# Two fillings of 96 and 32 bytes ahead of a transformer kernel's row buffers and second memory area

## The chip, the cores and the metric

The kernel runs on one core of a Trainium2 chip. The metric is the device time of one execution in microseconds. Before the change it is 1265.22 us, the median of three runs (1264.64 to 1267.24).

## What is computed

Two transformer blocks, one after the other, over 256 tokens of width 1024. The first has an mLSTM mixer and a layer of 16,384 experts (PEER); the second has a mixer of attention and a linear recurrence, and a plain MLP. The part that matters here is the expert layer. For each token and each of 8 heads, 16 experts are chosen, and each expert is one row of `u` and one of `v`:

```python
def block(args):
    hb, eb, gb = args
    ub = jnp.take(u, eb, axis=0)
    z = jnp.einsum('thkd,td->thk', ub, hb)
    a = (jax.nn.gelu(z.astype(jnp.float32)) * gb).astype(hb.dtype)
    return jnp.einsum('thk,thkd->td', a, jnp.take(v, eb, axis=0))
```

That is 256 x 128 rows of `u` and as many of `v`, all float32, 268 MB in all.

## The kernel before

It is written by hand with a program for each engine and semaphores between them. There are three stages that matter here.

**First block's mixer (to about 330 us).** SyncE streams the weights in loads of 1 MB (128 partitions x 8,192 bytes), most of them into five ring buffers `ring0` to `ring4`; three of the first loads go to `ya`, `qkT` and `pad`, which are not in use yet. ScalarE (L1073) and VectorE (L1550) split each chunk into a high and a low part, `halves`, and TensorE multiplies them with `hh` and `hl` (L496, L497, L500).

**Expert layer (about 320 to 965 us).** `peer_uv` holds for each expert its row of `u` and its row of `v` side by side, 8,192 bytes. GpSimd issues 256 gathers (L2398, the last three in two parts at L2407), each an indirect DMA of one expert for each of 128 tokens, so 1 MB into one row buffer. For each row buffer VectorE multiplies the `u` half with the token's `h2t` and sums (`dot`, L2042), ScalarE applies the gelu and writes a diagonal matrix `dg` (L1356), and TensorE adds the `v` half to the output in two products, which the trace has as two passes each (L858). There are 17 row buffers, in a list `row_places`:

```python
row_places = [gbuf[:, j, :] for j in range(4)] + [wq_places[j][:, :] for j in w_free[0:2]] + [ring[UV_SLOTS[2]][:, :]]
row_places += [gbuf[:, j, :] for j in range(4, 8)]
row_places += [row_place[:, :], ring[A0][:, :], ring[A1][:, :], wq_places[w_free[2]][:, :]]
row_places += [ring[j][:, :] for j in UV_SLOTS[0:2]]
```

So buffers 0 to 3 and 7 to 10 lie in `gbuf`, 4, 5 and 14 are the three `wq_place`, 11 is `row_place`, and 6, 12, 13, 15 and 16 are ring buffers. A table `ROW_SLOT` sets which gather goes where. From gather 94 to gather 157 its cycle has 16 gathers, in the order 4, 5, 8, 13, 14, 9, 0, 10, 15, 1, 2, 3, 6, 11, 7, 12; from gather 158 on buffer 16 stands behind 10 and the cycle has 17, to 216, where buffer 11 leaves. Three in each cycle go to a `wq_place`, one to `row_place`. A gather is issued as soon as TensorE is done with the row that the buffer held (semaphore `s_comb`). Of the 256 rows 50 go to the `wq_place` buffers, 15 to `row_place`, 126 to `gbuf` and 65 to the ring.

**Second block (965 us to the end).** Weights again through the ring, split into `half2_*`, and multiplied with `hf2`, `mxh`, `gh` and so on (L1017, L1020, L1047 to L1049).

SBUF tensors lie one behind the other in each partition, in the order in which the program names them, and each starts at a multiple of 32 bytes. Those named through `sb(...)` keep their place for the whole program. Behind them lies an area that is laid out anew for each stage (`st(...)`, given back by `stage.close()`): first the mixer's tiles, then the expert layer's, then the second block's.

Of the kernel before, what the change touches and what calls it, by code (L numbers as in the profile page):

```python
# [130 lines left out]
def build_program(nc, A, out):  # L131
# [6 lines left out]
    def sb(name, shape, dt=f32):  # L138
        return ctx.enter_context(nc.sbuf_tensor(name, shape, dt))
# [135 lines left out]
    iota16 = sb("iota16", [128, 16])  # L275
    mneg = sb("mneg", [128, 128], bf16)
    identb = sb("identb", [128, 128], bf16)
    banks = [ctx.enter_context(nc.psum_tensor(f"bank{i}", [128, 512], f32)) for i in range(8)]

    stage = ExitStack()  # L280

    def st(name, shape, dt=f32):
        return stage.enter_context(nc.sbuf_tensor(name, shape, dt))
# [38 lines left out]
    sct = st("sct", [128, 2, 4, 128])  # L322
    pk = st("pk", [128, 1088])
    rx = st("rx", [128, 3, 40])
    pku = st("pku", [128, 64], u32)
    ei = st("ei", [128, 2, 128], u32)
    za = st("za", [128, 2, 32])
# [2180 lines left out]
```

## Time and profile before

| | |
|---|---|
| median of three runs | 1265.22 us |
| the profiled execution: time | 1264.27 us |
| the profiled execution: span | 1262.5 us |
| TensorE matmul busy | 1142.1 us (90%) |
| VectorE busy | 919.4 us (73%) |
| ScalarE busy | 511.4 us (41%) |
| GpSimd busy | 328.7 us (26%) |
| moved by DMA | 406.70 MB, 322 GB/s over the span |

The span is the time from the first to the last instruction of the profiled execution. A share of 90% for TensorE is an average over stages: whether TensorE sets the time has to be read stage by stage, from the busy shares in slices or stretches of the span and from what the DMA engines do in the same stretch.

### The profile page before, as it was taken

What the parts mean: (1) busy time and instruction counts of PE and PEld (TensorE: products, weight loads), DVE (VectorE), ACT (ScalarE), POOL (GpSimd) and SP (SyncE); (2) the same over time, 40 slices, a digit from 0 to 9 for tenths busy, and PEclk for the clock granted to TensorE, in tenths of its full rate; (3) what the DMA queues carried; (4) which work ended last, traced back from release to release, by engine and by line L of the source; (5) the groups of instructions that cost most, each with busy time, mean ns of one, the idle gap of its engine ahead of it and who ended that gap; (6) DMA issues with size and microseconds to landing.
All of it is one profiled execution on the core that took longest, in us unless ns stands there. A gap on an engine that the chain in (4) does not pass through costs nothing.

```text
span 1262.5 us, 14930 instructions
## 1 busy us (share of the span) xinstructions
PE 1142.1 (90%) x5180; PEld 797.5 (63%) x5180; DVE 919.4 (73%) x1848; ACT 511.4 (41%) x992; POOL 328.7 (26%) x316
## 2 busy tenths in 40 slices
PE   5999999999899998988778878887789999999998
PEld 4989999998655454443333433332335897788887
DVE  5997987786869667777677766677756696888544
ACT  3657443554423222221222222221524477677442
POOL 4000000000446444544454454454433000000000
PEclk9999999999999999999998999899989999999999
DMA  8874577588999999999999999999997622555550
GB/s 352 335 283 185 179 293 279 208 318 325 363 424 393 426 424 426 426 426 425 426 426 426 425 426 426 426 426 425 427 423 309 232 101 73 195 195 176 197 200 34
DMA packets 58703, 406.70 MB, mean 322 GB/s; under 512 B 7012, under 2 KB 7220, under 8 KB 10500
## 3 DMA queue, kind: packets, MB, share of 16 engines
q0 software_dynamic: 39184, 273.55, 51.9%
q1 hardware_dynamic: 19444, 132.19, 28.3%
q8 instruction: 42, 0.69, 0.2%
q14 instruction: 33, 0.27, 0.1%
HBM read 404.66 MB, written 1.06 MB: 321 GB/s over the span
## 4 chain that ended last, share of the span: by engine, by line
PE 58%; DMA 25%; DVE 9%; issue 4%; ACT 3%; POOL 1%; SPq 0%; DVEq 0%; POOLq 0%; ACTq 0%
PE bank L858 15%; DMA row_place<-in_peer_uv,ei 8%; DMA ring<-in_peer_uv,ei 6%; PE bank L496 5%; PE bank L500 5%; PE bank L497 5%; DMA gbuf<-in_peer_uv,ei 5%; PE bank L1017 5%; DMA wq_place<-in_peer_uv,ei 4%; PE bank L781 3%; PE bank L1020 2%; PE bank L1047 2%; PE bank L1048 2%; PE bank L1049 2%; PE bank L521 2%
## 5 line engine op out<-in xcount | busy, mean ns | idle before, releaser
L858 PE MATMUL bank<-gbuf,dg 128*128 128x512 f32 x504 | 247.2, 632 | 60.2 <-ACT dg L1356 58.1
L1550 DVE TENSOR_TENSOR half<-ring,half 128x1024 fp32r<-128x1024 f32 x175 | 212.7, 1222 | 85.1 <-ACT half L1073 83.1
L1073 ACT ACTIVATE half<-ring 128x1024 fp32r<-128x1024 f32 x173 | 181.7, 1055 | 126.4 <-PE bank L1049 47.0
L858 PEld LDWEIGHTS bank<-gbuf,dg 128*128 128x128 f32 x504 | 98.1, 200 | 193.9 <-issue 112.6
L2042 DVE CUSTOM_DVE_ANT_0 gbuf<-gbuf,h2t 128x1024 f32<-128x1024 f32 x126 | 154.4, 1225 | 72.2 <-DMA gbuf<-in_peer_uv,ei 68.1
L2398 POOL DMA_INDIRECT gbuf<-in_peer_uv,ei x123 | 140.4, 1141 | 172.7 <-PE bank L858 107.7
L1348 ACT ACTIVATE za<-za 128x4 f32<-128x4 f32 x62 | 12.7, 205 | 401.9 <-DVE za L2042 401.9
L858 PE MATMUL bank<-ring,dg 128*128 128x512 f32 x260 | 131.1, 633 | 17.3 <-ACT dg L1356 13.0
L496 PE MATMUL bank<-hh,half 128*128 128x256 f32 x448 | 113.1, 290 | 0.6 <-DVE hl L1708 0.3
L2042 DVE CUSTOM_DVE_ANT_0 ring<-ring,h2t 128x1024 f32<-128x1024 f32 x65 | 79.7, 1225 | 46.5 <-DMA ring<-in_peer_uv,ei 43.9
L497 PE MATMUL bank<-hl,half 128*128 128x256 f32 x448 | 110.5, 284 | 0.0
L858 PEld LDWEIGHTS bank<-ring,dg 128*128 128x128 f32 x260 | 53.0, 207 | 88.1 <-issue 70.0
L2398 POOL DMA_INDIRECT ring<-in_peer_uv,ei x65 | 82.3, 1266 | 93.5 <-PE bank L858 44.0
L858 PE MATMUL bank<-wq_place,dg 128*128 128x512 f32 x200 | 96.5, 619 | 9.6 <-ACT dg L1356 6.8
L1356 ACT ACTIVATE dg<-ident,za 128x128 f32<-128x128 f32 x256 | 83.1, 391 | 40.4 <-DVE za L2053 29.9
L2398 POOL DMA_INDIRECT wq_place<-in_peer_uv,ei x50 | 59.1, 1181 | 111.3 <-DVE ei L1968 66.6
L496 PEld LDWEIGHTS bank<-hh,half 128*128 128x128 f32 x448 | 86.5, 193 | 1.5 <-issue 0.8
L497 PEld LDWEIGHTS bank<-hl,half 128*128 128x128 f32 x448 | 86.5, 193 | 0.5 <-issue 0.5
L2042 DVE CUSTOM_DVE_ANT_0 wq_place<-wq_place,h2t 128x1024 f32<-128x1024 f32 x50 | 60.9, 1224 | 22.0 <-DMA wq_place<-in_peer_uv,ei 20.1
L858 PEld LDWEIGHTS bank<-wq_place,dg 128*128 128x128 f32 x200 | 38.8, 197 | 59.0 <-issue 49.7
L1017 PE MATMUL bank<-hf,half 128*128 128x512 f32 x256 | 64.9, 394 | 0.1
L500 PE MATMUL bank<-hh,half 128*128 128x256 f32 x448 | 62.9, 283 | 0.0
(446 smaller groups left out, 1999.7 us busy)
## 6 DMA issues: line engine op xcount, KB each, us to landing
ring<-in_weights SPq DMA_DIRECT2D x116, 1024.0 KB, 5.3
gbuf<-in_weights SPq DMA_DIRECT2D x4, 1024.0 KB, 9.8
gbuf<-in_peer_uv,ei POOLq DMA_INDIRECT x129, 14.8
bcs<-in_b_ada POOLq DMA_DIRECT2D x3, 512.0 KB, 12.3
ring<-in_peer_uv,ei POOLq DMA_INDIRECT x65
xs<-in_x SPq DMA_DIRECT2D x2, 512.0 KB, 4.0
ya<-in_weights SPq DMA_DIRECT2D x1, 1024.0 KB, 18.0
qkT<-in_weights SPq DMA_DIRECT2D x1, 1024.0 KB, 20.0
```

The costliest lines, as they stand in the source:

```text
L496: e.matmul(pb[:, 0:256], hi[:, k, :], xh[:, k, :], start=k == 0, stop=False)
L497: e.matmul(pb[:, 0:256], hi[:, k, :], xl_[:, k, :], start=False, stop=False)
L500: r = e.matmul(pb[:, 0:256], lo[:, k, :], xh[:, k, :], start=False, stop=k == 7)
L521: r = e.matmul(two[a][:, :], xh[:, k, 128 * a:128 * a + 128], lo[:, k - k0, :], start=False, stop=stop and k > k0)
L781: r = e.matmul(pb[:, s_], v[:, k, :], hf[:, k, s_], start=k == 0, stop=k == 7)
L858: r = e.matmul(acc[a][j][:, :], dg[:, i % 4, :], expert_rows(i)[:, 1024 + 512 * j:1536 + 512 * j], start=h == 0 and k == 0, stop=h == 7 an ...
L1017: e.matmul(pb[:, :], hi[:, k, :], hf2[:, :, k, :], start=k == 0, stop=False)
L1073: e.activation(h, v, AF.Copy).then_inc(*o.inc(*highs_of(n)))
L1356: e.activation(dg[:, i % 4, :], ident[:, :], AF.Copy, scale=za[:, i // 16 % 2, 16 + i % 16:17 + i % 16]).then_inc(*o.inc(s_dg, i + 1))
L1550: e.tensor_tensor(l, v, h.bitcast(f32), ALU.subtract).then_inc(*o.inc(s_lov, split(n)))
L2042: e.tensor_tensor_reduce(row, row, h2t[:, ITS[n][0], :], 1.0, 0.0, ALU.mult, ALU.add, za[:, n % 2, i % 16:i % 16 + 1]).then_inc(*o.inc(s_d ...
L2398: e.indirect_dma_start(out=expert_rows(i), out_offset=None, in_=A["peer_uv"], in_offset=bass.IndirectOffsetOnAxis(ap=ei[:, a, at:at + 1], ...
```

## The change

Two tensors are added that no instruction reads or writes.

```diff
     identb = sb("identb", [128, 128], bf16)
+    sb("to_line0", [128, 24])
     banks = [ctx.enter_context(nc.psum_tensor(f"bank{i}", [128, 512], f32)) for i in range(8)]
...
     rx = st("rx", [128, 3, 40])
+    st("to_line1", [128, 8])
     pku = st("pku", [128, 64], u32)
```

The first takes 96 bytes of each partition, behind the lasting tensors; everything of the three stages' area moves up by 96 bytes. The second takes 32 bytes between `rx` and `pku` in the expert layer's area; what lies behind it there moves by 128 bytes in all. No instruction is added, removed or reordered on any engine or queue, and no size changes. What changes is where tensors start in a partition. The offset of the start from a multiple of 256 bytes, before and after:

| tensors | before | after |
|---|---|---|
| `ring0` to `ring4`, `xs`, `bc0`, `bcs`, `ident`, `masks` | 128 | 128 |
| `wq_place0` to `2` (row buffers 14, 4 and 5), `row_place` (buffer 11) | 32 | 128 |
| `gbuf` (row buffers 0 to 3 and 7 to 10), `dg`, `ei` | 0 | 128 |
| `hf`, `h2t`, `qT`, `skT`, `sct`, `pk` | 32 | 128 |
| first mixer: `halves`, `hh`, `hl`, `yh`, `yl`, `pad` | 32 | 128 |
| first mixer: `cg`, `qkT`, `vx`, `wo_half*` | 160 | 0 |
| first mixer: `ya`, `xn`, `scr`, `accd`, `nb` | 224 | 64 |
| second block: `half2_*`, `hf2`, `xn3`, `mxh`, `mxl`, `gh`, `gl_` | 32 | 128 |
| second block: `xl`, `gl`, `rg`, `ig`, `tmp`, `w1`, `wbd`, `mixT` | 96 | 192 |

So in the expert layer every row buffer starts at 128 beyond a multiple of 256 after the change, as those in the ring do before it.

## Rows read from the trace of the kernel before

**Rows 1.** The page's head, and busy time, share and instructions of each engine.

```profile
span 1262.5 us, 14930 instructions
PE 1142.1 (90%) x5180; PEld 797.5 (63%) x5180; DVE 919.4 (73%) x1848; ACT 511.4 (41%) x992; POOL 328.7 (26%) x316
```

**Rows 2.** Stages: stretch, its length, busy us of each engine, PEclk, DMA share, GB/s.

```profile
33.00:331.00 298.00, 295.09 (x2214) 279.65 (x2213) 245.35 (x403) 160.12 (x272) 13.27 (x17) 1.00 0.71 268
600.00:700.00 100.00, 79.78 (x182) 35.47 (x181) 69.14 (x170) 24.48 (x64) 45.29 (x38) 0.93 1.01 426
700.00:800.00 100.00, 81.69 (x193) 36.82 (x192) 72.92 (x191) 22.10 (x61) 50.40 (x44) 0.94 1.01 426
965.00:1262.50 297.50, 288.10 (x1536) 243.65 (x1534) 202.06 (x277) 174.01 (x268) 4.82 (x9) 1.00 0.46 161
```

**Rows 3.** Same view: the six gathers from buffer 4 on, then the cycle's rest.

```profile
575.60:590.50 14.90, 11.90 (x23) 4.98 (x24) 10.39 (x29) 2.40 (x9) 6.96 (x6) 0.89 1.01 423
590.50:615.10 24.60, 18.33 (x42) 7.43 (x40) 17.75 (x42) 6.10 (x15) 13.81 (x12) 1.00 1.01 428
615.10:629.90 14.80, 12.71 (x25) 5.36 (x26) 10.22 (x28) 2.80 (x10) 5.62 (x5) 0.88 1.01 426
629.90:654.40 24.50, 18.41 (x48) 8.11 (x46) 18.15 (x45) 6.56 (x16) 13.36 (x12) 1.00 1.01 427
...
735.80:750.70 14.90, 11.99 (x29) 5.18 (x28) 9.62 (x29) 1.48 (x5) 7.51 (x7) 1.00 1.01 424
750.70:777.70 27.00, 20.74 (x50) 9.04 (x49) 19.20 (x45) 7.90 (x20) 11.96 (x10) 0.94 1.01 427
777.70:792.60 14.90, 11.69 (x27) 4.67 (x25) 11.17 (x32) 1.48 (x5) 9.11 (x7) 1.00 1.01 422
792.60:819.60 27.00, 21.18 (x39) 8.98 (x40) 18.43 (x43) 7.53 (x19) 11.04 (x9) 0.81 1.01 427
```

**Rows 4.** Same view: three gathers each, to buffers 6, 11 and 7.

```profile
644.61:651.97 7.36, 6.42 (x15) 2.96 (x16) 5.00 (x11) 4.26 (x9) 3.49 (x4) 1.00 1.01 427
684.16:691.52 7.36, 7.36 (x18) 3.23 (x17) 5.19 (x13) 4.45 (x9) 5.78 (x5) 1.00 1.01 427
```

**Rows 5.** Same view: three gathers each, to buffers 1, 2 and 3.

```profile
637.25:644.61 7.36, 5.92 (x14) 2.28 (x12) 5.87 (x16) 0.28 (x2) 4.04 (x4) 1.00 1.01 427
760.48:767.84 7.36, 6.68 (x16) 2.74 (x16) 5.86 (x13) 3.02 (x8) 3.14 (x3) 1.00 1.01 427
```

**Rows 6.** Row buffers' instructions, by tile: count, duration ns min/median/max, first and last start.

```profile
L858 PE MATMUL bank<-row_place,dg x60: 592/592/1061, 359.3 to 871.3; 128*128 128x512 f32 x60
L858 PE MATMUL bank<-ring,dg x260: 592/592/1220, 354.1 to 960.8; 128*128 128x512 f32 x130
L858 PE MATMUL bank<-gbuf,dg x504: 592/592/1222, 343.8 to 965.9; 128*128 128x512 f32 x168
L2042 DVE CUSTOM_DVE_ANT_0 ring<-ring,h2t x65: 1206/1225/1292, 345.4 to 954.0; 128x1024 f32<-128x1024 f32 x65
L2042 DVE CUSTOM_DVE_ANT_0 wq_place<-wq_place,h2t x50: 1215/1225/1226, 330.3 to 912.6; 128x1024 f32<-128x1024 f32 x50
L2042 DVE CUSTOM_DVE_ANT_0 gbuf<-gbuf,h2t x126: 1204/1225/1292, 333.7 to 958.9; 128x1024 f32<-128x1024 f32 x126
```

**Rows 7.** Groups by line and form: busy us, mean ns, then idle before.

```profile
L661 PE MATMUL bank<-accd,ones_f 128*128 128x512 f32 x16 | 7.5, 592 | 0.0
L1550 DVE TENSOR_TENSOR half<-ring,half 128x1024 fp32r<-128x1024 f32 x175 | 212.7, 1222 | 85.1 <-ACT half L1073 83.1
L1550 DVE TENSOR_TENSOR wo_half<-ring,wo_half 128x1024 fp32r<-128x1024 f32 x4 | 4.9, 1220 | 0.5 <-ACT wo_half L1073 0.5
L1610 DVE TENSOR_TENSOR yl<-ya,yh 128x256 fp32r<-128x256 f32 x16 | 6.7, 417 | 0.3 <-ACT yh L1234 0.2
```

**Rows 8.** First stretch, in the view by stretches, and its longest step of the last chain.

```profile
0.00:33.00 33.00, 17.71 (x80) 17.04 (x80) 18.06 (x22) 10.89 (x15) 14.35 (x39) 1.00 0.90 356
...
6.16 17.95 DMA ya<-in_weights
```

## The prediction

> **What bounds the kernel now.** I read the stages before the averages. TensorE's 90% [rows 1] is not one number. In the first mixer, from 33 to 331 us, TensorE is busy 295.09 of 298.00 us, and in the second block 288.10 of 297.50 us, with the DMA engines at 0.71 and 0.46 [rows 2]: both stages end when TensorE does. The expert layer is the other way round: in two stretches of 100 us TensorE is busy 79.78 and 81.69 us, VectorE 69.14 and 72.92 us, while the DMA share stands at 1.01 and the rate at 426 GB/s in both [rows 2]. There the gathers set the time. One gather moves 128 x 8,192 bytes = 1.049 MB, which at 426 GB/s is 2.46 us, and 256 of them take 630 us, half of the program. So an edit that moves row buffers counts only if it changes the time per gather; an edit that moves matmul operands counts only if it changes matmul durations in the outer two stages.
>
> **Does the place of a row buffer matter today?** The cycle of the buffers lets the trace answer in part. I cut the expert layer where the row for buffer 4 begins to arrive: six gathers (buffers 4, 5, 8, 13, 14, 9, of which 4, 5 and 14 are the `wq_place` at 32 beyond a multiple of 256), then the ten or eleven others of the cycle. The reader is to see the last column go up and down: 423, 426, 424 and 422 GB/s in the shown six-gather stretches, 428, 427, 427 and 427 in the rest [rows 3]. I read eight such pairs; the four not shown have 423, 426, 424, 422 against 427, 427, 427, 428. Means: 423.75 and 427.25, so 0.82% less. Of 14.86 us (the mean length of the short stretches) this is 0.12 us per cycle. Charged to the three `wq_place` rows it is 0.04 us each, 1.6% of a gather.
>
> But `row_place`, buffer 11, starts at the same 32 beyond a multiple of 256, and the stretches of three gathers that hold its row run at 427 GB/s [rows 4], as those of three `gbuf` rows do [rows 5]. Of the five stretches of buffers 6, 11 and 7 that I read, one has 426 and four 427; of five of buffers 1, 2, 3 all have 427. If the 32-byte offset by itself cost 1.6% of a gather, one row of three would show as 0.5%, or 2 GB/s. It does not. So the loss goes with the `wq_place` buffers, or with their place in the cycle, and not plainly with their offset. The ring rows (128 beyond) and the `gbuf` rows (0 beyond) cannot be told apart: the fast stretches hold both.
>
> **The change part by part.**
>
> 1. *Instructions.* None is added, removed or moved on any engine or queue, SP's and POOL's among them, and there is no new wait. Cost 0.
> 2. *The 50 rows of the `wq_place` buffers.* They go from 32 to 128 beyond. Ends: nothing, if the loss is not one of the offset; 50 x 0.04 = 2.0 us saved, if all of it is. Because DMA is the bound, a saving here would reach the end: TensorE has 18 to 20 us of slack in each 100 [rows 2] and would be late next only after that is used up. I take the end of nothing, because the nearest row, that of `row_place` at the same offset [rows 4], shows no loss to be had back. Both ends stay.
> 3. *The 15 rows of `row_place`.* No loss now [rows 4], none to gain: 0. The rate's resolution is 1 of 427 GB/s in three rows, 0.017 us per row, so +-0.3 us for 15.
> 4. *The 126 rows of `gbuf`.* They go from 0 to 128 beyond, the offset at which the 65 ring rows stand already. Stretches that hold ring and `gbuf` rows and stretches of `gbuf` rows alone have the same 427 [rows 3, 5]: 0. Ends: if a row at 128 cost what one at the `wq_place` costs (0.04 us), +5.0 us; below, the rate's resolution of 1 in 427 leaves -0.7 us.
> 5. *Reads and writes by the engines in the expert layer.* VectorE's dot takes 1225 ns (median) with its row at 128 (ring), at 32 (`wq_place`) and at 0 (`gbuf`), and TensorE's product 592 ns at 32 (`row_place`), 128 and 0 [rows 6]. 0, and with DMA as the cover it would be hidden anyway up to some 18 us in each 100.
> 6. *Operands in the two outer stages.* Here TensorE has no cover: its 295.09 + 288.10 = 583 us are the path [rows 2]. The products there are of another type (fp32r), with both operands at 32 beyond in nearly all cases, so no row shows one with aligned operands. The nearest rows: the f32 product of 512 columns has 592 ns at offsets 0, 32, 128 [rows 6] and 224 (`accd`) [rows 7]. Equal to the nanosecond, so the bound is 1 in 592, which on 583 us is +-1.0 us. VectorE's split takes 1222 ns into `half` (32) and 1220 into `wo_half` (160) [rows 7], and its mean idle before it is ScalarE's doing. I take 0 and keep +-1.0 us.
> 7. *The first loads.* The chain begins with the load into `ya`, 17.95 us [rows 8], which moves from 224 to 64 beyond; `qkT` and `pad` move too. Three loads at the first stretch's 356 GB/s are 8.8 us; 1.6% of that is 0.14 us either way. I take 0.
>
> Sum against the profiled execution: 1264.27 + 0 = 1264.3 us, its own time (1.8 us of it lie around the span). The median of the runs is 0.95 us above it, so against the median the forecast is 1265.2 us.
>
> The Trainium skill speaks against the change in one place. The page "DMA: Bandwidth & Descriptors", section "How a descriptor splits into AXI transactions", says that a transaction must start at a multiple of 256 bytes, and that the bytes fetched ahead of an unaligned start cost beats of 32 bytes. Counted so, an estimate from that page, a row of 8,192 bytes takes 256 beats at offset 0, 257 at 32 and 260 at 128: `gbuf` rows would get 1.6% dearer. The fast stretches, in which ring rows at 128 run at the rate of `gbuf` rows [rows 3, 5], do not agree.
>
> **The rivals.**
>
> *A, nothing changes* (the forecast): parts 2 to 7 at the values taken, 1265.2 us.
>
> *B, the `wq_place` rows are freed.* For it: the loss recurs in every cycle [rows 3], and these buffers are moved onto the offset of buffers without it. Against it: `row_place` [rows 4]. Time: 1265.2 - 2.0 = 1263.2 us.
>
> *C, slower: the row buffers in `gbuf` leave their multiple of 256.* One mechanism: a write that starts at 128 beyond needs an extra piece, and the DMA engines, which have no idle time to put it in, pass it on. Place: the 126 `gbuf` rows. Price: 0.04 us each, as above, +5.0 us: 1270.2 us. It decides as soon as it is more than 0.02 us per row, since 126 x 0.02 = 2.5 us. For it: nothing but that DMA is full, so that any extra time shows. Against it: [rows 3, 5], and 65 ring rows that run so already. That is the page's rule above as a mechanism of this kernel; by its beats, 126 rows x 1.6% and 65 x 1.2% of 2.46 us would give +6.9 us, 1272.1 us.
>
> *D, faster: TensorE's fp32r products, or the reads behind them, gain from aligned operands.* No row speaks for it, and the f32 rows speak against it; no fp32r row has aligned operands. Were it 1% of 583 us it would be -5.8 us: 1259.4 us.
>
> *E, the change doesn't do what it says.* The row buffers do come to 128 beyond, but not to a multiple of 256, and the second block's `xl` to `mixT` only to 64 modulo 128. For the time this is case A.
>
> **How the numbers follow.** A measurement of this kernel can tell about 0.2% from no change, which is 2.5 us. Chances: A with E 0.55, B 0.27, C 0.08, D 0.10. A and B both lie within 0.2% at their own prices; B's 2.0 us is close enough to 2.5 that I give a sixth of it to "faster". Within 0.2%: 0.55 + 0.22 = 0.77. Faster: 0.10 + 0.05 = 0.15. Slower: C, 0.08. The predicted time is A's, 1265.2 us. The range: A with +1.0 us of part 6 and the 2.0 us by which the highest of the three runs stands over their median (1267.24 against 1265.22) reaches to 1268.2; B with -1.0 us and the 0.6 us of the lowest run (1264.64) goes down to 1261.6. Together they hold 0.82 of the chance, which is what is wanted, so C and D stay outside: 1261.5 to 1268.2.
>
> **What the profile would show.** If A is right, the saw of 423 to 427 GB/s between the two parts of the cycle stays, and the cycle of 16 keeps its 39.3 to 39.5 us. If B is right, the six-gather stretches run at 427 and the expert layer ends 2 us sooner, with both outer stages unchanged. If C is right, all stretches fall by 4 to 7 GB/s. If D is right, the mean of L496, L497 and L1017 falls and the end of the first mixer comes sooner. The forecast is wrong if the DMA rate in 600 to 800 us leaves 426 by more than 2, or if a product's duration moves by more than 1 ns in 290.

## The result

The changed kernel takes 1271.78 us (median of 7 runs, 1269.93 to 1273.84) against 1265.41 us for the kernel before in the same measurement (7 runs, 1264.64 to 1267.24): ratio 1.0048, 95% interval 1.0039 to 1.0058. It is 6.4 us slower. The forecast was 1265.2 us, with 1261.5 to 1268.2 as range and "slower" at 0.08. The profiled execution has a span of 1270.1 us, 7.6 us more than in [rows 1].

The page's head and busy times of the changed kernel:

```profile
span 1270.1 us, 14930 instructions
PE 1147.8 (90%) x5180; PEld 801.2 (63%) x5180; DVE 920.0 (72%) x1848; ACT 511.5 (40%) x992; POOL 327.9 (26%) x316
```

The stretches of [rows 2], and the cycle parts of [rows 3], in the changed kernel (stretch, its length, busy us of each engine, PEclk, DMA share, GB/s):

```profile
33.00:331.00 298.00, 294.50 (x2210) 278.87 (x2210) 245.37 (x403) 160.23 (x272) 13.51 (x18) 1.00 0.71 268
600.00:700.00 100.00, 82.83 (x184) 36.31 (x183) 70.07 (x176) 23.96 (x62) 44.83 (x39) 0.91 1.01 421
700.00:800.00 100.00, 79.70 (x192) 35.98 (x192) 70.65 (x181) 21.79 (x60) 50.52 (x43) 0.97 1.01 421
...
619.90:634.80 14.90, 11.66 (x22) 4.90 (x23) 10.39 (x29) 2.58 (x9) 5.65 (x5) 0.83 1.01 422
634.80:659.60 24.80, 20.55 (x52) 9.01 (x50) 18.04 (x43) 6.86 (x17) 13.71 (x12) 0.97 1.01 421
...
784.30:799.30 15.00, 11.16 (x26) 4.48 (x24) 11.30 (x32) 1.49 (x5) 8.79 (x8) 1.00 1.01 419
799.30:826.70 27.40, 19.04 (x38) 8.08 (x39) 17.96 (x43) 7.42 (x19) 12.30 (x10) 0.89 1.01 421
```

The first mixer is as it was: TensorE busy 294.50 of 298 us against 295.09. The expert layer is not. Its DMA share is still 1.01, so the gathers still set the time, but they now move 421 GB/s instead of 426, and the saw of [rows 3] is gone: where 423 and 427 alternated, both parts of the cycle lie at 418 to 422. Both have come down, the fast one most, to below what the slow one had. At 1.049 MB a gather takes 2.491 us instead of 2.462 us; over 256 gathers that is 7.5 us, against 7.6 us between the spans. The rates are rounded to 1 GB/s, so this sum is good to about 1.5 us and no better.

The same instructions as in [rows 6, 7], by tile and by form:

```profile
L2044 DVE CUSTOM_DVE_ANT_0 gbuf<-gbuf,h2t x126: 1206/1225/1286, 333.2 to 967.3; 128x1024 f32<-128x1024 f32 x126
...
L860 PE MATMUL bank<-row_place,dg x60: 592/592/697, 362.0 to 878.4; 128*128 128x512 f32 x60
...
L1552 DVE TENSOR_TENSOR half<-ring,half 128x1024 fp32r<-128x1024 f32 x175 | 212.8, 1222 | 85.6 <-ACT half L1075 83.6
L498 PE MATMUL bank<-hh,half 128*128 128x256 f32 x448 | 113.0, 290 | 0.6 <-DVE hl L1710 0.3 <-ACT vx L1179 0.2
L499 PE MATMUL bank<-hl,half 128*128 128x256 f32 x448 | 110.5, 284 | 0.0
```

The dot is at 1225 ns, the pass of 512 columns at 592, the split at 1222, as before, and the fp32r products of the first mixer at 290 and 284 ns as before. In the second block the mean of the products of L1017 (now L1019) went from 394 to 398 ns, but their median is 393 in both, and x1 below, whose operands there have not moved, has 398 too. So no duration changed with the place of the operands. The last dot on a `gbuf` row starts at 967.3 instead of 958.9 us, while the first starts at 333.2 instead of 333.7 us [rows 6]: the time is lost between the first gather and the last.

So the question is what a row buffer's start does to a gather. One thing in the result is odd. The five ring buffers have not moved, 128 beyond a multiple of 256 before and after. Yet their rows lay in stretches of 427 GB/s before, and no stretch runs at that rate now.

### The profile page after: what moved, and what is told of

It reads as the page before. It is cut to its first block, busy times and chain, and to the rows that moved or that the text cites. A ratio compares the mean times of both kernels' runs of the same rounds, so it can differ in the third digit from the quotient of the medians.

```text
span 1270.1 us, 14930 instructions
## 1 busy us (share of the span) xinstructions
PE 1147.8 (90%) x5180; PEld 801.2 (63%) x5180; DVE 920.0 (72%) x1848; ACT 511.5 (40%) x992; POOL 327.9 (26%) x316
## 4 chain that ended last, share of the span: by engine, by line
PE 55%; DMA 26%; DVE 8%; issue 5%; ACT 3%; POOL 2%; SPq 0%; POOLq 0%; DVEq 0%; ACTq 0%
PE bank L860 12%; DMA row_place<-in_peer_uv,ei 10%; DMA ring<-in_peer_uv,ei 6%; PE bank L498 5%; PE bank L502 5%; PE bank L499 5%; DMA gbuf<-in_peer_uv,ei 5%; PE bank L1019 5%; DMA wq_place<-in_peer_uv,ei 4%; PE bank L783 3%; PE bank L1022 2%; PE bank L1051 2%; PE bank L1049 2%; PE bank L1050 2%; PE bank L523 2%
## 5 line engine op out<-in xcount | busy, mean ns | idle before, releaser
L860 PE MATMUL bank<-gbuf,dg 128*128 128x512 f32 x504 | 253.0, 645 | 58.0 <-ACT dg L1358 56.8
L1552 DVE TENSOR_TENSOR half<-ring,half 128x1024 fp32r<-128x1024 f32 x175 | 212.8, 1222 | 85.6 <-ACT half L1075 83.6
L1075 ACT ACTIVATE half<-ring 128x1024 fp32r<-128x1024 f32 x173 | 181.8, 1056 | 128.3 <-PE bank L1051 47.0
L2044 DVE CUSTOM_DVE_ANT_0 gbuf<-gbuf,h2t 128x1024 f32<-128x1024 f32 x126 | 154.3, 1225 | 77.6 <-DMA gbuf<-in_peer_uv,ei 74.5
L860 PE MATMUL bank<-wq_place,dg 128*128 128x512 f32 x200 | 93.9, 606 | 12.6 <-ACT dg L1358 11.5
L2044 DVE CUSTOM_DVE_ANT_0 wq_place<-wq_place,h2t 128x1024 f32<-128x1024 f32 x50 | 61.0, 1225 | 21.7 <-DMA wq_place<-in_peer_uv,ei 20.4
L1019 PE MATMUL bank<-hf,half 128*128 128x512 f32 x256 | 65.8, 398 | 0.1
```

Source lines behind the costliest of these rows:

```text
L860: r = e.matmul(acc[a][j][:, :], dg[:, i % 4, :], expert_rows(i)[:, 1024 + 512 * j:1536 + 512 * j], start=h == 0 and k == 0, stop=h == 7 an ...
L1019: e.matmul(pb[:, :], hi[:, k, :], hf2[:, :, k, :], start=k == 0, stop=False)
L1075: e.activation(h, v, AF.Copy).then_inc(*o.inc(*highs_of(n)))
L1552: e.tensor_tensor(l, v, h.bitcast(f32), ALU.subtract).then_inc(*o.inc(s_lov, split(n)))
L2044: e.tensor_tensor_reduce(row, row, h2t[:, ITS[n][0], :], 1.0, 0.0, ALU.mult, ALU.add, za[:, n % 2, i % 16:i % 16 + 1]).then_inc(*o.inc(s_d ...
```

## The theory, and the experiments

**Theory W (write side with a store).** This is a guess made after the result, from the old trace; the runs below test it. In it the DMA engines read a row at a fixed pace. In the trace of the kernel before, undisturbed gathers follow each other at 2453 ns, and those to buffers 5 and 14 land about 2485 ns after the one ahead of them (2.46 to 2.54 us). "Off" stands below for a start that is no multiple of 256 bytes. A row whose buffer starts off a multiple of 256 bytes takes the write side longer than the read pace, one at a multiple takes less. The difference is kept in a store, and shows only when this is full. Fitted to where the slow gathers lie in the old cycle: an off row adds 32 ns, a row at a multiple takes 26 ns out, the store holds some 110 ns. It would explain the saw, and the result: 256 off rows at 32 ns are 8.2 us, against 1.1 us that it gives for the kernel before, so 7.1 us more where 6.4 us were measured. In the order 12, 4, 5, 8, 13, 14, 9 the rows 12, 4, 5, 13, 14 are off and fill it; 1, 2, 3 and 9, 0, 10 empty it, so that 6 and 11 (`row_place`) find it empty and are free.

The rivals, with letters of their own (B and E here are not the B and E of the prediction): E, some other moved tensor is to blame (`ei`, `dg`, `hf`, operands); N, each off row pays by itself; P, it is the `wq_place` buffers themselves; B, the price goes by the bytes ahead of the start.

The experiments are fillings in the kernel before. Each was timed in turns with the kernel before on the same chip, whose median was 1263.86 us with x1 to x4, 1264.11 us with x5 to x8 and 1262.98 us with the last two, so times are to be compared by their ratio to it. The ratios are those on record, each with its 95% interval; the quotient of two medians differs from them by up to 0.1%.

**x1: `gbuf` alone.**

```diff
     g3 = st("g3", [128, D])
+    st("to_gbuf", [128, 32])
     gbuf = st("gbuf", [128, NGB, 2048])
```

> The kernel before with one filling of 128 bytes directly ahead of gbuf, so that gbuf alone moves, from 0 to 128 beyond a multiple of 256. Theory W (a gather's row that starts off a multiple of 256 takes the write side longer, about 2485 ns a row, than the 2453 ns at which rows are read; rows at a multiple take less; the difference is stored up to some 110 ns and shows only when the store is full): all 17 row buffers are now off, so the whole of the loss, about +6.4 us, 1271.8, and 421 GB/s in all of 600 to 800 us. Rival E (the loss comes from another moved tensor: ei, dg, hf, h2t or the operands of the outer stages): 1265.4 and 426 GB/s.

Measured: 1271.52 us, ratio 1.0070 (1.0056 to 1.0084). The profile of x1 has, in the view by stretches:

```profile
600.00:700.00 100.00, 81.42 (x179) 35.90 (x178) 68.50 (x169) 24.56 (x64) 46.08 (x38) 0.90 1.01 421
700.00:800.00 100.00, 80.68 (x195) 36.48 (x194) 71.90 (x188) 22.23 (x61) 50.37 (x43) 0.96 1.01 421
```

The one filling makes the whole loss, with every other tensor where it was. (Its ratio is even a little above the 1.0048 of the change, which was measured in another series; the rate, 421 GB/s, is the same.) Rival E falls.

**x2: all but `gbuf`.**

```diff
+    sb("to_line0", [128, 24])
...
+    st("to_line1", [128, 8])
...
+    st("to_gbuf", [128, 32])
     gbuf = st("gbuf", [128, NGB, 2048])
```

> The changed kernel with a further 128 bytes ahead of gbuf, so that gbuf is back at a multiple of 256 and all else stays as changed (wq_place and row_place at 128 beyond). Theory W, if 128 and 32 beyond cost the same: 1265.4, with the saw of 423 to 427 GB/s back. Rival E: 1271.8 and 421 GB/s. If 32 and 128 differ in price, something between 1264 and 1267.

Measured: 1263.66 us, ratio 0.9995 (0.9983 to 1.0008). From the view by stretches of x2, two six-gather parts and what follows each:

```profile
778.50:793.40 14.90, 12.00 (x25) 5.04 (x24) 11.29 (x32) 1.48 (x5) 7.58 (x6) 0.89 1.01 423
793.40:820.50 27.10, 19.97 (x46) 8.17 (x45) 18.27 (x43) 7.41 (x19) 14.22 (x11) 1.00 1.01 427
820.50:835.20 14.70, 9.82 (x23) 3.85 (x21) 11.71 (x35) 1.69 (x6) 8.21 (x8) 1.00 1.01 425
835.20:862.30 27.10, 21.26 (x45) 8.96 (x46) 18.46 (x43) 7.21 (x18) 11.89 (x11) 0.94 1.01 427
```

The time is that of the kernel before, and the saw is back, flatter: over eleven cycles the six-gather parts have 425.2 GB/s on average, against 423.8 before, the rest 427.2 in both. Two executions of one kernel (x3 and y1 below) differ by 0.4 in this average, so the step from 423.8 is more than that: off by 128 costs somewhat less than off by 32. In the time it doesn't show (-0.6 us, interval -2.2 to +1.0). All other tensors, with the operands of the outer stages, are worth nothing that can be measured.

**x3: all row buffers at a multiple of 256.**

```diff
+    sb("to_ring", [128, 32])
     ring = [sb(f"ring{i}", [128, 2048]) for i in range(NS)]
...
+    sb("to_line0", [128, 24])
...
+    st("to_gbuf", [128, 8])
     gbuf = st("gbuf", [128, NGB, 2048])
```

> Fillings put all 17 row buffers, ring included, at a multiple of 256. Theory W with its store: the gathers run at 427 to 428 GB/s throughout, and only the 1 to 2 us are won that the six-gather stretches lose before: 1263.4 to 1264.4. Rival N (no store: every row off a multiple costs the same by itself, 6.4 us / 126 rows = 0.051 us): the 130 rows that are off before would give back 6.6 us: 1258.8 and over 430 GB/s.

Measured: 1261.15 us, ratio 0.9988 (0.9976 to 1.0001), which is 1.5 us less, with 3.0 us less as the far end. The view by stretches of x3:

```profile
600.00:700.00 100.00, 81.93 (x189) 36.28 (x188) 70.04 (x171) 24.48 (x64) 44.72 (x38) 0.95 1.01 427
700.00:800.00 100.00, 82.02 (x195) 36.79 (x193) 73.90 (x194) 21.99 (x61) 53.45 (x46) 0.95 1.01 427
```

The slow parts rise (426.4 on average over eleven cycles, the rest 427.0), and nothing rises above 428, where the upper parts were already. Rival N wanted 1258.8 us, 6.6 us less, and over 430 GB/s, and falls in this form; the rate has a ceiling at 427, which is the read side's in theory W. A form of N with that ceiling but no store, in which each off row takes 32 ns more than the ceiling allows, would have won 130 x 32 ns = 4.2 us here. That too lies outside the interval.

**x4 and x5: all row buffers at 32, and at 224 beyond.** As x3, with `to_ring` of 160 and of 96 bytes.

> Fillings put all 17 row buffers at 32 beyond a multiple of 256. Theory W, if the extra piece of a write is what costs, whatever its size: as the changed kernel, 1271.8 and 421 GB/s. Rival B (cost by the bytes ahead of the start: 32 instead of 128, a quarter of the price, 8 of 32 ns a row, for which the read side leaves room): at or below the kernel before, 1264 to 1266 and 426 to 428 GB/s. By the rule of the Trainium skill's page DMA: Bandwidth & Descriptors, section How a descriptor splits into AXI transactions, the start at 32 costs one beat of 32 bytes and the start at 128 four.

> Fillings put all 17 row buffers at 224 beyond a multiple of 256. Theory W with a price per extra piece: 420 to 421 GB/s in 600 to 800 us, as at 32 and 128. Rival B (a price by the bytes between the 256-byte line and the start, seven beats of 32 bytes): 7 beats on 256 is 2.7%, so 415 GB/s or less. A third way, by the bytes up to the next line (32 instead of 224): better than at 32.

Measured: x4 1272.17 us, ratio 1.0071 (1.0056 to 1.0086); x5 one execution, 1271.82 us. The view by stretches, of x4 first:

```profile
600.00:700.00 100.00, 77.16 (x186) 34.36 (x185) 70.82 (x178) 24.48 (x64) 52.31 (x40) 0.98 1.01 420
```

and of x5:

```profile
600.00:700.00 100.00, 77.71 (x184) 34.67 (x183) 69.69 (x175) 24.40 (x64) 48.45 (x38) 0.97 1.01 420
```

32, 224 and 128 beyond give 420, 420 and 421 GB/s. The price is for being off a multiple of 256, nearly whatever the distance, and the middle one is slightly the cheapest. Rival B falls. Only starts at 0, 32, 128, 160 and 224 beyond were run. The Trainium skill's page "DMA: Bandwidth & Descriptors", section "How a descriptor splits into AXI transactions", is borne out in its line at 256 bytes: worked out from it, an estimate, a row off the line needs 33 transactions instead of 32. It is not borne out in its count of beats, by which 32 beyond would cost one, 128 four and 224 seven.

**x6: half of `gbuf` off.**

```diff
-    gbuf = st("gbuf", [128, NGB, 2048])
+    gbuf = st("gbuf", [128, 4, 2048])
+    st("to_gbuf", [128, 32])
+    gbuf_hi = st("gbuf_hi", [128, 4, 2048])
```

> The kernel before with gbuf cut in two by a filling of 128 bytes: buffers 0 to 3 stay at a multiple of 256, 7 to 10 move to 128 beyond. Theory W with a store (an off row adds 32 ns to it, a row at a multiple takes 26 ns out, it holds some 110 ns): worked out over the table of buffers, the extra is 3.9 us against 1.1 before: +2.8 us on the kernel before of the same chip. The saw deepens: 421 to 422 GB/s in the six gathers from buffer 4 on (all but none of them at a multiple), 425 to 426 in the rest of the cycle. Rival N (each off row pays by itself): the 54 rows that move, of 126 whose move costs 6.9 us, are 3.0 us, but spread by the counts: 7 of 10 or 11 rows against 6 of 6 off, so no stretch at 427.

Measured: 1266.15 us, ratio 1.0017 (1.0004 to 1.0030), which is +2.1 us. From the view by stretches of x6:

```profile
600.00:700.00 100.00, 81.08 (x185) 36.02 (x184) 70.07 (x177) 24.31 (x65) 45.71 (x38) 0.93 1.01 424
700.00:800.00 100.00, 79.24 (x193) 35.88 (x192) 71.55 (x185) 21.93 (x62) 51.04 (x43) 0.97 1.01 422
...
656.80:671.80 15.00, 13.95 (x41) 7.52 (x40) 10.23 (x29) 3.24 (x11) 8.27 (x6) 1.00 1.01 420
671.80:696.50 24.70, 20.05 (x43) 8.26 (x41) 17.96 (x44) 5.94 (x14) 11.58 (x10) 0.93 1.01 425
...
781.00:796.00 15.00, 12.00 (x25) 5.07 (x24) 10.73 (x30) 1.48 (x5) 7.03 (x6) 0.89 1.01 421
796.00:823.20 27.20, 21.32 (x45) 8.69 (x44) 18.39 (x43) 7.42 (x19) 13.31 (x12) 0.94 1.01 425
```

The averages over eleven cycles are 421.2 and 425.0 GB/s, as expected (421 to 422 and 425 to 426). The time doesn't decide here: the interval, +0.5 to +3.8 us, holds W's 2.8 us and rival N's 3.0 us. It also follows that the step comes in parts: not all of the loss needs all of `gbuf`.

**x7: the ring at a multiple, `wq_place` and `row_place` off it.** This is the kernel that separates W from P. Buffers 4, 5 and 14 are still off, but at 160 beyond instead of 32; the ring rows in front of them no longer are. So two things have changed for them. A kernel with every row at 160 was not run, so that this distance costs at all is not shown; 32, 128 and 224 do when every row has them.

```diff
+    sb("to_ring", [128, 32])
     ring = [sb(f"ring{i}", [128, 2048]) for i in range(NS)]
...
+    st("to_gbuf", [128, 32])
     gbuf = st("gbuf", [128, NGB, 2048])
```

> ring and gbuf at a multiple of 256, wq_place and row_place (65 rows) at 160 beyond, so that buffers 4, 5 and 14 stay off but the ring rows 12 and 13 ahead of them no longer are. Theory W with a store: the store never fills (sum 0.0 us), the six-gather stretches run at 427 like the rest, and the time is that of all rows at a multiple: about 1.1 to 2 us under the kernel before. Rival P (it is the wq_place buffers themselves that are slow when off): the six-gather stretches stay at 423 to 424 and the time at that of the kernel before.

Measured: 1261.92 us, ratio 0.9986 (0.9975 to 0.9997). From the view by stretches of x7:

```profile
600.00:700.00 100.00, 79.31 (x186) 35.12 (x186) 69.16 (x171) 24.48 (x64) 43.22 (x36) 0.97 1.01 427
...
613.70:628.40 14.70, 11.57 (x23) 4.86 (x24) 10.40 (x29) 2.55 (x9) 5.59 (x5) 0.88 1.01 427
628.40:653.00 24.60, 19.55 (x51) 8.61 (x49) 17.98 (x43) 6.99 (x18) 14.12 (x12) 1.00 1.01 428
...
776.00:790.90 14.90, 10.83 (x25) 4.29 (x23) 11.35 (x32) 1.48 (x5) 8.74 (x8) 1.00 1.01 424
790.90:817.90 27.00, 20.97 (x44) 8.95 (x45) 17.54 (x44) 7.41 (x19) 12.55 (x11) 0.94 1.01 427
```

Over eleven cycles it is 425.9 against 427.3 GB/s, where it was 423.8 against 427.2. Four single parts still fall to 422 to 425, as two fall to 424 in x3, where no row is off; the reading by single gathers below shows that these are a few disturbed gathers, and that the saw is gone. The 65 off rows cost nothing that the time can tell: it is that of x3 within 1 us, with intervals of about +-1.5 us on both.

**x8: the ring alone off** (`to_line0` of 224 bytes, `to_gbuf` of 32).

> wq_place, row_place and gbuf at a multiple of 256, the ring at 128 beyond as before (65 rows off, singly or in pairs). Theory W with a store: no loss, 427 GB/s throughout, the time of all rows at a multiple: 1 to 2 us under the kernel before. Rival N: 65 off rows keep their 0.05 us each: 3 us more than with all rows at a multiple, and 425 GB/s.

Measured: 1261.67 us, ratio 0.9983 (0.9969 to 0.9998). The view by stretches of x8:

```profile
600.00:700.00 100.00, 82.15 (x186) 36.18 (x185) 69.91 (x175) 24.49 (x64) 43.93 (x38) 0.93 1.01 427
700.00:800.00 100.00, 81.87 (x191) 36.84 (x190) 72.89 (x190) 22.00 (x61) 50.85 (x44) 0.93 1.01 427
```

Again 65 off rows for nothing: a price per row would leave 425 GB/s and cost 3 us against x3. x7 and x8 have one half each of what the kernel before has together, and neither half has a saw. This is what a store does and a price per row does not.

**The best version once more, and a dip put elsewhere.** The first is the kernel of x3. The second is x6's edit together with `to_ring` of 128 bytes, so that buffers 0 to 3 are off and 7 to 10 are at a multiple.

> All 17 row buffers at a multiple of 256 once more, for the interval. Theory W: 1 to 2 us under the kernel before of the same chip, ratio 0.9985 to 0.999; the first run of it gave 0.9988.

> ring and buffers 7 to 10 at a multiple of 256, wq_place and row_place at 160 beyond, buffers 0 to 3 at 128 beyond: 137 rows off, 7 more than before. Theory W with a store: by the table of buffers, off rows are never more than two in a row but for 1, 2, 3, so the six gathers from buffer 4 on lose nearly nothing (above 425 GB/s) and the small dip stands in the rest of the cycle, around buffer 3; in all 1.2 us lost against 1.1 before, so the time of the kernel before within 1 us. Rival N (each off row pays by itself): 0.05 us x 7 more than before, and the six gathers, of which buffers 4, 5 and 14 are off, lose as much per row as the rest.

Measured: 1261.13 us, ratio 0.9991 (0.9979 to 1.0002), and 1261.81 us, ratio 0.9991 (0.9981 to 1.0001). y2 has 137 rows off, 7 more than the kernel before, and is not slower than it (the expectation was its time within 1 us; it came 1.1 us lower). From its view by stretches:

```profile
613.50:628.30 14.80, 12.55 (x25) 5.34 (x26) 10.24 (x31) 2.97 (x10) 5.60 (x5) 0.88 1.02 430
628.30:652.90 24.60, 18.57 (x48) 8.12 (x47) 18.28 (x45) 6.47 (x16) 13.51 (x12) 1.00 1.01 426
...
817.80:832.50 14.70, 11.93 (x28) 4.78 (x26) 11.33 (x33) 1.62 (x6) 8.39 (x8) 1.00 1.01 428
832.50:859.70 27.20, 22.70 (x48) 9.47 (x48) 18.58 (x43) 7.28 (x19) 13.36 (x12) 0.94 1.01 426
```

The six-gather parts, which had 423.8 in the kernel before, have 426.3 on average and the rest 426.5. The dip has all but left the six gathers, of which three are still off.

**Read by single gathers.** The kept traces have the end of every DMA packet. The table has the time in ns from the last packet of one gather to the last packet of the next, as the median over the gathers to one buffer (gathers 94 to 213, six to eight for each); a star marks an off row, and the columns stand in the order of the cycle (10, 16 and 15, between 0 and 1, are left out). Packets of neighbouring gathers overlap, so a delay may show one gather late.

| | 1 | 2 | 3 | 6 | 11 | 7 | 12 | 4 | 5 | 8 | 13 | 14 | 9 | 0 |
|---|---|---|---|---|---|---|---|---|---|---|---|---|---|---|
| before | 2453 | 2453 | 2453 | 2453* | 2453* | 2453 | 2453* | 2453* | 2453* | 2480 | 2473* | 2460* | 2479 | 2462 |
| x2 | 2453 | 2453 | 2453 | 2453* | 2453* | 2453 | 2453* | 2453* | 2453* | 2464 | 2453* | 2455* | 2463 | 2457 |
| x6 | 2474 | 2454 | 2453 | 2453* | 2453* | 2453* | 2468* | 2484* | 2492* | 2491* | 2485* | 2489* | 2487* | 2473 |
| y2 | 2453* | 2453* | 2453* | 2462 | 2453* | 2453 | 2453 | 2453* | 2453* | 2456 | 2458 | 2453* | 2453 | 2453* |

In x3, y1, x7 and x8 each of these medians is 2453; what keeps their averages below the ceiling are 13 to 17 gathers of 120 that take up to 175 ns longer, in x3 and y1, where no row is off, as well. With all rows off by 128 (the changed kernel) the medians are 2482 to 2493, with all off by 32 or 224 (x4, x5) about 2492 to 2502.

So off rows go free where at most two stand together, as in x7 and x8. Up to three in a row go free too (6, 11, 7 in x6; 12, 4, 5 in the kernel before; 1, 2, 3 in y2), and the delay begins right behind the third: at 12 in x6, at 8 in the kernel before, at 6 in y2. The delay also outlasts the off rows: buffers 9 and 0 of the kernel before are both at a multiple, and the gather to 0 still takes 2462 ns. A price that each off row pays by itself can do neither.

## Why the prediction was wrong

**Right:** that DMA bounds the expert layer and TensorE the outer two stages; that the engines' own durations would not move (parts 5 and 6: 1225, 592, 290 and 284 ns, unchanged; in x2, where all but `gbuf` moves, the time is 0.6 us less, inside the bound of +-1.0 us, though its interval reaches -2.2); that any change in the time per gather reaches the end (7.5 us by the rate, 7.6 us in the span); that the six-gather parts hold a loss worth up to some 2 us (x3, y1, x7 and x8 win 1.1 to 2.1 us by giving it back, though the intervals of x3 and y1 just reach 0). The sign that was named for being wrong came: the rate in 600 to 800 us left 426 by 5.

**Wrong, the step that failed: part 4,** "Stretches that hold ring and `gbuf` rows and stretches of `gbuf` rows alone have the same 427 [rows 3, 5]: 0". The reading was right, the conclusion was not: the term that was put at 0 measured +6.4 us. It took the time of a row as belonging to that row alone. Ring rows were free because `gbuf` rows at a multiple of 256 stood between them and the others. The 126 rows that the change moved were the ones that gave this cover, and with them moved the ring rows lost it: gathers to buffers 6 and 12, which did not move, went from 2453 to 2482 and 2485 ns (medians). x1 shows the move of `gbuf` alone to be the cause (421 GB/s, +0.70%), and x8 that the same ring rows are free where all others are at a multiple (427 GB/s).

**Wrong for the same reason: part 2,** where `row_place`, off like `wq_place` but without a loss, was taken as evidence against the offset. Its position in the cycle, behind three `gbuf` rows and one ring row, protected it. x7 shows that the `wq_place` rows are free as well once the ring rows ahead of them are at a multiple. The gain of the prediction's rival B would not have come even with `gbuf` left alone: x2 does that, and the six-gather parts rise from 423.8 to 425.2 GB/s, not to the 427 that B wanted; 128 beyond is still off. The loss was also charged to three `wq_place` rows alone, while buffer 13, a ring row in the same six gathers, is off as well.

**Rival C was the case** in its place and its direction, and its price of 0.04 us per `gbuf` row gave +5.0 us where +6.4 us came (6.4 / 126 = 0.051 us). It had half of the mechanism: the moved rows become off rows, but they also stop covering the others, which C didn't have. The price was taken from the average of six gathers, of which several were still protected. Its sign, all stretches down by 4 to 7 GB/s, came in the fast parts, which fell by 5 to 7; the six-gather parts fell by 2 to 4. That it got 0.08 was the fault: the one sign named for it, "DMA is full, so that any extra time shows", was stronger than the two rows against it, because those could not see a cost that is covered. The rule from the Trainium skill's page "DMA: Bandwidth & Descriptors", section "How a descriptor splits into AXI transactions", that a start off 256 bytes costs, was put aside on the same rows. By its beats it gave 1272.1 us, an estimate. That is within 0.4 us of the measured time by luck and not by what it counts, as x4 and x5 show.

**Open:** what the store is. The runs show its effect, not the part of the chip; that it sits on the write side is argued from the fact that only destinations moved. The three numbers of the fit (32, 26, 110 ns) were fitted on the kernel before and then foretold x6, x7, x8 and y2 in rough size; they were not measured one by one. The 32 ns for an off row is borne out by the changed kernel (2487 against 2453 ns, medians of 120 gathers); at 32 and 224 beyond it is nearer 40 ns (2493), which the fit leaves out. Nor is it known why 128 beyond is cheaper than 32 and 224.

## What to carry to other kernels

If DMA bounds a stage, look where the destination rows start in a partition: here a start off a multiple of 256 bytes cost 1.4 to 1.6% of the rate when all rows had it (421 and 420 against 427 GB/s), and a multiple of 128 was not enough. Off rows were free here as long as no more than two or three stood together with rows at a multiple between them. So a row without a loss in the profile says nothing of what it costs when its neighbours change, and a neutral-looking edit has to be judged by what it does to the cover of the others.

## What the runs showed of the hardware

- The rate of gathers into SBUF has a ceiling of 427 GB/s here, which all destinations at a multiple of 256 bytes reach and do not pass (x3), and a floor of 420 to 421 with all of them off (the changed kernel, x1, x4, x5). Undisturbed, a gather of 1.049 MB takes 2453 ns in the first case, about 2487 ns off by 128 bytes, 2493 ns off by 32 or 224 (medians).
- The distance from the multiple hardly matters: 32 and 224 bytes gave 420 GB/s, 128 bytes 421.
- A mix of both can be better than the mean of both. With 65 of 256 rows off, 427 GB/s (x7, x8), where the mean by rows would be 425 to 426; with 184 off, 422 to 424 (x6), about the mean.
- Three off rows in a row cost nothing, and the delay begins with the gather behind them (before, x6, y2).
- The starts of matmul, VectorE and ScalarE operands, moved by 96 or 128 bytes throughout, changed no duration that the profile shows: 592, 290 and 284 ns, 1225 and 1222 ns, and 1055 and 1056 ns for ScalarE's split.
